# Tiles 1 to 3 of the mixer scanned in one pass, its output sums and the expert choices planned apart, a single tile's choice decoded in halves

## The reference, cut to what matters

```
y_ssd  = group_rmsnorm(y * silu(z)) @ ssd_w_out          # 8 groups of 256
y_sc   = (sb * causal_dwconv(sc * sx)) @ sc_w_out
merged = sigmoid(gates[:D]) * y_ssd + sigmoid(gates[D:]) * y_sc
h      = h + merged @ w_o
q = (rmsnorm(h) @ w_q)  -> 8 heads, 2 halves of 128
s = q . sub_keys        -> 128 scores per half; top 16 of each half,
                           then the top 16 of the 16 x 16 sums
eidx, g = indices and softmax of the 16 chosen (8 heads: 128 experts per token)
act = gelu(x . expert_u[eidx]);  h = h + sum(g * act * expert_v[eidx])
```

## Time and profile before

| | |
|---|---|
| median of three runs | 2622.79 us (2622.34 to 2625.23) |
| the profiled execution's own time | 2603.1 us |
| its span | 2601.3 us |
| TensorE busy | 2228.9 us (86%) |
| VectorE busy | 1518.6 us (58%) |
| GpSimd busy (gathers) | 1018.1 us (39%) |
| ScalarE busy | 686.5 us (26%) |
| moved by DMA | 869.29 MB, mean 334 GB/s |
| mean granted clock of TensorE | 0.924 of full speed |

### The profile page before, as it was taken

The page is one execution under the profiler, slowest core; times in us unless marked ns, Lnnn a source line. Parts: engine busy times, 40 slices in busy tenths (PEclk is TensorE's granted clock), DMA queues, the critical chain, the costliest instruction groups (busy, mean ns, idle before and its releaser), DMA issues.

```text
span 2601.3 us, 31972 instructions
## 1 busy us (share of the span) xinstructions
PE 2228.9 (86%) x11976; PEld 1677.5 (64%) x11976; DVE 1518.6 (58%) x3603; ACT 686.5 (26%) x2063; POOL 1018.1 (39%) x1028
## 2 busy tenths in 40 slices
PE   7999889988859999899868753468989799999998
PEld 7998778986758888678534133323365555546695
DVE  3441185854698998866643678841047678675210
ACT  6662245621225555400101010011022100001320
POOL 0000003333334564445456665666644556572000
PEclk9999999989879999899989977689997899999999
DMA  6556658999788998799999998999989999997375
GB/s 231 222 211 220 258 220 342 406 373 410 269 317 330 388 398 335 279 393 414 367 358 411 377 346 352 380 410 353 387 335 351 369 400 396 414 406 297 136 300 205
DMA packets 186091, 869.29 MB, mean 334 GB/s; under 512 B 20800, under 2 KB 21056, under 8 KB 153680
## 3 DMA queue, kind: packets, MB, share of 16 engines
q0 software_dynamic: 147456, 536.94, 53.4%
q1 hardware_dynamic: 37904, 328.20, 32.4%
q10 hardware_dynamic: 576, 2.10, 0.2%
HBM read 865.06 MB, written 2.10 MB: 333 GB/s over the span
## 4 chain that ended last, share of the span: by engine, by line
PE 69%; DVE 16%; issue 5%; ACT 4%; DMA 3%; another core or an unknown queue 2%; POOL 1%; DVEq 0%; ACTq 0%
PE ps L995 68%; DVE rows L2332 8%; POOL rows L975 1%; DMA rows<-in_pv,eidxT 1%; DMA wr<-in_wso 1%; ACT ynT L1631 1%; DVE si L1879 0%; PE ps L1340 0%; DVE tmpx L1965 0%; DVE h L2356 0%; PE ps L1104 0%; DMA wr<-in_wqku 0%; DVE late L1877 0%; DVE wb L2191 0%
## 5 line engine op out<-in xcount | busy, mean ns | idle before, releaser
L975 POOL DMA_INDIRECT rows<-in_pu,eidx x512 | 485.0, 947 | 982.1 <-DVE dots L2332 441.8
L2332 DVE CUSTOM_DVE_ANT_0 rows<-rows,ps 128x1024 f32<-128x1024 f32 x512 | 593.5, 1216 | 6.5 <-issue 5.9
L995 PE MATMUL ps<-uT,wr 128*128 128x128 f32 (+3 forms) x3456 | 553.6, 318 | 17.4 <-issue 11.1
L995 PEld LDWEIGHTS ps<-uT,wr 128*128 128x128 f32 x3456 | 502.6, 195 | 52.4 <-issue 18.9
L995 PE MATMUL ps<-hT,wr 128*128 128x128 f32 (+2 forms) x1600 | 363.9, 388 | 38.0 <-issue 34.2
L975 POOL DMA_INDIRECT rows<-in_pv,eidx x256 | 289.7, 1132 | 216.4 <-DVE h L2356 110.7
L995 PEld LDWEIGHTS ps<-hT,wr 128*128 128x128 f32 x1600 | 262.3, 199 | 135.5 <-issue 40.7
L975 POOL DMA_INDIRECT rows<-in_pv,eidxT x256 | 243.2, 950 | 144.8 <-issue 60.7
L995 PE MATMUL ps<-rows,wz 128*32 128x512 f32 x1024 | 207.8, 632 | 30.2 <-DMA rows<-in_pv,eidxT 24.4
L2356 DVE SCALAR_TENSOR_TENSOR h<-rows,wgt,h 128x1024 f32<-128x1024 f32 x132 | 169.1, 1281 | 5.0 <-DMA rows<-in_pv,eidx 4.1
L2356 DVE SCALAR_TENSOR_TENSOR ps<-rows,wgt,ps 128x1024 f32<-128x1024 f32 x122 | 156.7, 1285 | 11.2 <-DMA rows<-in_pv,eidx 10.9
(11 more groups left out here) (409 smaller groups left out, 2827.1 us busy)
## 6 DMA issues: line engine op xcount, KB each, us to landing
wr<-in_wg SPq DMA_DIRECT2D x48, 1536.0 KB
wr<-in_wsc SPq DMA_DIRECT2D x24, 1536.0 KB
wr<-in_wso SPq DMA_DIRECT2D x24, 1536.0 KB
wr<-in_wgu SPq DMA_DIRECT2D x33, 1024.0 KB
wr<-in_wgate SPq DMA_DIRECT2D x24, 1024.0 KB
wr<-in_wqku SPq DMA_DIRECT2D x15, 1024.0 KB
wr<-in_wo SPq DMA_DIRECT2D x12, 1024.0 KB
wr<-in_wdn SPq DMA_DIRECT2D x8, 1536.0 KB
```

The costliest lines, as they stand in the source:

```text
L975: e.indirect_dma_start(ring[i % NR], None, A[table], bass.IndirectOffsetOnAxis(ap=index[:, t, k:k + 1], axis=0)).then_inc(gathered[i % NR] ...
L995: return e.matmul(o, l, r, start=start, stop=stop, skip_group_check=True)
L2332: e.tensor_tensor_reduce(row, row, wide[:], 1.0, 0.0, MUL, ADD, dots[:, k:k + 1]).then_inc(*dve.up(*u))
```

## The change

- `SCANS = ((0, 1), (1, 4))`: tiles 1, 2 and 3 are scanned in one pass of 384 columns, over the weights of `in_wg` and `in_wsc` once. `GROUPS` keeps the three groups for the sums (`plan_sum`) and the choices.
- `scan(g)` goes chunk by chunk: `inside(c)` of one chunk, then `across(c - 1)` of the one before; its chunk buffers are two sets in turn (`c % 2`) in place of one per chunk, and `before_chunk` names the chunk whose reader must be done. z comes in two products (two chunks and one).
- The order: scan 0, sum 0, choice 0 merged with scan 1, sum 1, then choice 1 merged with sum 2, choice 2.
- In a sum, 4, 3 or 2 pairs of gate products (`AHEAD_GATES`) are made before the transposes, into as many buffers; both gates of a j share one bank and one sigmoid, both output products one bank and one multiplication. `yturn` fills a bank with four transposes. Queries and scores of a head come out of PSUM two at a time.
- `PIECES = (2, 2, 1)`: for tiles 0 and 1 the decoding is done for heads 0 to 3 after head 4's `top`, and for heads 4 to 7 at the end; a gather of the first 64 rows of expert_u waits for the first half alone.
- The scan of tiles 1 to 3 keeps some of its buffers in ring slots 8 to 12, as does choice 1. Until tile 1's choice is decoded the ring of rows has 8 slots, then 13. Working memory of the first block is one arena.
- Weight slots are 4 of 2304 values in place of 3 of 3072. `in_wg` comes in 3 pieces of 1 MB in place of 2 of 1.5 MB, `in_wsc` and `in_wso` in a piece of 1 MB and one of 0.5 MB, `in_wdn` in pieces of 4 (last 2) in place of 6 (last 4) rows of blocks. The pieces used at the end of the kernel have 4 slots more in place of 3.
- `QUOTA`, `CX`, `CY` and `SX` have other values.

```diff
-WSLOT = 3072
+WSLOT = 2304
-NW = 3
+NW = 4
-MIXERS = ((0, 1), (1, 2), (2, 4))
+SCANS = ((0, 1), (1, 4))
+GROUPS = ((0, 1), (1, 2), (2, 4))
-SX = 1.6
-PLACES = ("early", "beside", "ring")
-CX = 3.1
-CY = 1.7
+SX = 1.8
+PLACES = ("early", "ring", "ring")
+CX = 5.3
+CY = 4.4
+NR0 = 8
+AHEAD_GATES = (4, 3, 2)
+GATE_BUFFERS = (4, 3, 2)
+PIECES = (2, 2, 1)
-QUOTA = {('mixer', 1, 1): 17, ('mixer', 1, 2): 19, ('late', 1): 6, ('sum', 1): 26, ('mixer', 2, 0): 66, ('mixer', 2, 1): 62, ('mixer', 2, 2): 39, ('sum', 2): 82, ('query', 2): 98, ('top', 3): 65, ('attend', 0): 142, ('heads', 0): 64, ('wout', 0): 42, ('attend', 2): 20, ('heads', 2): 19, ('wout', 2): 4, ('feed', 0): 20, ('feed', 0, 0): 28, ('feed', 0, 1): 34, ('feed', 0, 2): 49, ('down', 0, 0): 35, ('down', 0, 1): 100, ('top', 2): 0, ('query', 1): 14, ('late', 2): 20, ('feed', 0, 3): 8, ('top', 0): 0, ('mixer', 1, 0): 0}
+QUOTA = {('query', 2): 108, ('top', 3): 72, ('attend', 0): 128, ('heads', 0): 66, ('wout', 0): 53, ('attend', 2): 20, ('heads', 2): 10, ('wout', 2): 8, ('feed', 0): 13, ('feed', 0, 0): 39, ('feed', 0, 1): 23, ('feed', 0, 2): 50, ('down', 0, 0): 25, ('down', 0, 1): 130, ('top', 2): 3, ('query', 1): 10, ('feed', 0, 3): 21, ('top', 0): 0, ('mixer', 1, 0): 0, ('mixer', 1, 1): 33, ('mixer', 1, 2): 34, ('mixer', 1, 3): 31, ('mixer', 1, 4): 28, ('mixer', 1, 5): 31, ('mixer', 1, 6): 35, ('mixer', 1, 7): 27, ('mixer', 1, 8): 3, ('late', 1): 5, ('sum', 1): 22, ('late', 2): 9, ('sum', 2): 74, ('top', 1): 5}
...
+def before_chunk(q, g, c):
+    n = len(group(*SCANS[q])[4])
+    if c >= 2:
+        return g, c - 2
+    return (g - 1, c + 2 * ((n - 1 - c) // 2)) if g else None
...
+        slopes(0)
+        slopes(1)
+        for c in range(nc_ + 1):
+            if c < nc_:
+                yield from inside(c)
+            if c:
+                yield from across(c - 1)
...
+    for j in range(AHEAD_GATES[q]):
+        yield from gate_products(j)
+    for i in range(4 * nt):
+        pl.take(("yturn", q, i), "lo", ("act", "yturn", q, i))
...
+    def decoded(t, h):
+        if PIECES[q] == 2 and h == 4:
+            yield from decode(t, 0)
...
-        yield from mixer[0]
-        yield from turns(mixer[1], choose[0])
-        yield from merge(pl, (choose[0], 0.001), (mixer[1], CX))
-        yield from turns(mixer[2], choose[1])
-        yield from merge(pl, (choose[1], 0.001), (until("clear", mixer[2]), CY))
-        yield from mixer[2]
+        yield from scan[0]
+        yield from sums[0]
+        yield from turns(scan[1], choose[0])
+        yield from merge(pl, (choose[0], 0.001), (scan[1], CX))
+        yield from sums[1]
+        pl.rings.update(lo=(0, 1), hi=(3, 4))
+        yield from merge(pl, (choose[1], 0.001), (sums[2], CY))
+        pl.rings.update(lo=(0, 1, 2), hi=(3, 4, 5))
         yield from choose[2]
...
-                w.wait_ge(*(act.at("index", t) if kind == "row" else dve.at("chosen", t)))
+                if kind == "row":
+                    w.wait_ge(*act.at("index", t))
+                else:
+                    w.wait_ge(*dve.at("chosen", t, 0 if kind == "dot" and k < 64 else pieces_of(t) - 1))
...
                 elif kind == "xdt":
+                    old = before_chunk(q, g, c)
+                    if old is not None:
+                        w.wait_ge(*pe.at("outer" if group(*SCANS[q])[4][old[1]][2] is None else "y", q, *old))
```

More of the change, by code:

```diff
@@ L107, in __init__ @@
         self.units, self.bank, self.slot, self.loads = [], {}, {}, []
-        self.held = {"ring": [], "early": [], "beside": [], "last": []}
+        self.held = {"ring": [], "early": [], "last": []}
         self.turns = ("ring",)
-        self.rings = {"lo": (0, 1, 2, 3), "hi": (4, 5, 6, 7), "six": (6,), "seven": (7,)}
+        self.rings = {"lo": (0, 1, 2, 3), "hi": (4, 5, 6, 7), "two": (2,), "five": (5,)}
         self.turn = {k: 0 for k in self.rings}
@@ L136, in load @@
         k = len(held)
-        first, n_ = {"ring": (0, NW), "early": (NW, 3), "beside": (NW + 3, 2), "last": (NW + 5, 3)}[place]
+        first, n_ = {"ring": (0, NW), "early": (NW, 3), "last": (NW + 3, 4)}[place]
         old = held[k - n_] if k >= n_ else ("dve", "h2e", NT - 1) if place == "last" else None
@@ L254, in scan, with slopes, inside @@
     def scan(g):
-        real = [(c, col, k) for c, (col, w_, k) in enumerate(chunks) if k is not None]
-        pl.add("slopes", q, g)
-        for c, (col, w_, k) in enumerate(chunks):
+        def slopes(c):
+            if c < nc_ and chunks[c][2] is not None:
+                pl.add("slopes", q, g, c)
+        def inside(c):
+            col, w_, k = chunks[c]
             pl.take(("back", q, g, c), "hi", ("act", "xdt", q, g, c))
@@ L843, in build @@
+        ob = ring[9:9 + NT]
+        wr += [rows[:, WSLOT * i:WSLOT * i + WSLOT] for i in range(4)]
         with ExitStack() as pk:
@@ L933, in build @@
         job_of = {u: i for i, u in enumerate(jobs)}
+        consumers = ("dot", "vrow", "rows")
+        narrow = NR0 + sum(2 if u[0] == "rows" else 1 for u in pl.units[:pl.units.index(("chosen", 1, 1, PIECES[1] - 1))]
+                           if u[0] in consumers)
+        slots, user, slot_of, before_of, value_of = [7, 5, 6, 0, 1, 2, 3, 4], {}, [], [], []
+        for i in range(len(jobs)):
+            if i == narrow:
+                slots = list(range(NR0, NR)) + slots
+            s = slots.pop(0)
+            slots.append(s)
+            slot_of.append(s)
+            before_of.append(user.get(s))
+            value_of.append(16 if user.get(s) is None else value_of[user[s]] + 16)
+            user[s] = i
         def sync(e):
@@ new lines, in gpsimd, with known @@
+            w.wait_ge(*pe.at("turn", ("mix", 0), SCANS[0][1]))
+            issued, chosen, used = 0, set(), -1
+            def known(i):
+                kind, t, k = jobs[i][0:3]
+                return (t, 0 if kind == "dot" and k < 64 else pieces_of(t) - 1) in chosen
+            for u in pl.units:
+                if u[0] == "chosen":
+                    chosen.add(u[2:4])
+                elif u[0] in consumers:
+                    used = job_of[("row", u[1], u[2], 2 * u[3] + 1) if u[0] == "rows" else u]
+                else:
+                    continue
+                while issued < len(jobs) and known(issued) and (
+                        before_of[issued] <= used if before_of[issued] is not None else
+                        slot_of[issued] < NR0 or (1, PIECES[1] - 1) in chosen):
+                    gather(issued)
+                    issued += 1
@@ L2110, in vector @@
                 elif kind == "slots":
-                    _, q, t = u
+                    _, q, t, piece = u
                     m = CH[q]
-                    i = t - MIXERS[q][0]
-                    cx, first, rd = m["cx1"], m["cx0"], m["rd"]
-                    gt = gate[:, t, :].rearrange("p (h k) -> p h k", h=8)
-                    unit, place, last, second = (m[f"cy{i_}"] for i_ in range(4))
+                    i = t - GROUPS[q][0]
+                    hs = heads_of(q, piece)
+                    mine = lambda nm: m[nm][:, 0:hs.stop - hs.start]
```

876 lines of the change are left out of this document (454 added, 422 removed).

## The result

The changed kernel took 2555.49 us (median of four runs, 2549.31 to 2565.66), the kernel before beside it 2624.01 us (2622.34 to 2626.77): ratio 0.9746, 95% interval 0.9717 to 0.9776. It is 68.5 us faster. The forecast was 2544, its range 2490 to 2610. (The median before is 2624.01 here and was 2622.79 in the prediction, because a fourth run came in.)

The account below looks back on a forecast made before the run. The prediction took TensorE and whatever makes it stop as the bound. Its terms -3 -95 -20 +12 +27 gave -79 us, so 2622.8 became 2544 us, with a whole range of 2490 to 2610.

Parts of the forecast that it names:

- Start to choice 0, -3: Start to 300 us: unchanged but for four gate pieces made ahead of tile 0's normalisation, -3 us (0 to -8).
- One scan, periods of 57.6: Scan of tiles 1 to 3: eight groups at TensorE's pace, each 57.6 us in place of 58.2.
- Sum of tile 1 ... I take 102, -20: Sum of tile 1: from 122 to 102 us, -20, bounds 92 and 122.
- Scans with choice 0, 613 to 518: Choice 0 and scans, with choice 1 moved out: 613 us become 518, -95, of which 493 is TensorE work.
- Sum 2 with choice 1, 242: Sum of tiles 2 and 3 with choice 1 inside: 230 us without it become 242, +12, bounds 206 and 260.
- Choice 2, +27: Choice 2, 258 us before: 20 rows missing at its start are made up there, +27 us, bounds 0 and +35.
- From 1523 on, 0: First attention stage and what follows: the same 1078 us, taken as 0 within -15 to +10.
- Saved traffic given back: Rival: DMA idles once tile 0's rows are finished and pays later in the sums and choice 2; 2582 us, chance 0.26.
- Everything packs: Rival: from 388 to 1523 us TensorE's work fills 95% of the time, saving 127 us; 2495 us, chance 0.14.
- The scan waits on its own chunks: Rival: two chunk buffer sets serve three chunks, stopping TensorE up to 4.0 us per chunk; 2640 us, chance 0.10.
- No change: Rival: the first attention stage waits for tile 1's last row, which comes no sooner; 2623 us, chance 0.06.
- near 1440: Sign of being right: the first attention stage would start near 1440 us.

Follow-up runs that it names:

- e6_rows_kept: Changed kernel with 28 rows of tile 0 moved from the scan to the start of the sum of tiles 2 and 3; 2504.65 us against 2483.67 unaltered, chip 10.
- e2_seek_late: Changed kernel, rows of tiles 0 and 1 sought only after both halves of the choice are decoded; 2564.03 us against 2556.34 unaltered, chip 5.
- e12_sum_light: Changed kernel with 20 rows moved from the sum of tiles 2 and 3 into choice 2; 2578.90 us against 2552.65 unaltered, chip 6.
- first pair: First traces of the kernel before and the changed kernel, medians 2624.01 and 2555.49 us; the second pair traces both kernels on chip 6, 2614.20 and 2552.65.
- e7_three_slots: Changed kernel with three weight slots of 2304 values in place of four; 2514.29 us against 2483.67 unaltered, chip 10.
- e4_traffic: Changed kernel with each weight piece of the scan of tiles 1 to 3 also copied memory to memory; 2588.48 us against 2556.34 unaltered, chip 5.
- e3_choice_alone: Changed kernel with choice 1 planned ahead of the sum of tiles 2 and 3, not beside it; 2570.28 us against 2556.34 unaltered, chip 5.
- e1_again: Changed kernel run again unaltered on chip 5; 2556.34 us against 2611.16 for the kernel before.
- e10_again: Changed kernel run again unaltered on chip 6; 2552.65 us against 2614.20 for the kernel before.

## Why the prediction came out as it did

The direction was right and the time in the range, 11 us above the forecast. That it came so near was partly luck: by its own steps one error of 48 us met others of the opposite sign.

- *Start to choice 0, -3.* It ended at 298.40 against 298.59: 0.
- *One scan, periods of 57.6.* 57.43. 58.2 - 57.43 = 0.8 us was saved in a group, where the constant of the rows had said 0.6 for 112 instructions; the order inside a group changed too, so the other 0.2 has no one cause. The prediction misread its own rows beside the page: by the Trainium skill's formula ("TensorE: Matmul & The Clock Gate", Back-to-back issue gap), N/2.4 ns plus 2.5 ns, an instruction of 128 columns would be spaced 0.056 us, and the earlier trace rows have 0.112. An estimate with that page's gap taken twice gives 0.112, 0.218 and 0.325 us, and the rows have 0.112, 0.216 and 0.322. So taken, the trace agrees with the page, and 112 x 5 ns = 0.6 us a group is the very term that the sum used; it is not 2 us, and no larger gap of small products is needed.
- *The failed step: "Sum of tile 1 ... I take 102, -20", and with it the cut of the windows.* The old windows were cut 18.3 us and 29.6 us ahead of the two scans' ends. The new lengths of both sums were then built from the sums' own work, 92 and 206 us of TensorE. So 47.9 us of scan (39.2 of them TensorE work, 14.1 + 25.1) stood on the side of before and nowhere on the side of after. At the true joint sum 1 was 104.1 us long, not 122, and it became 110.0: +6, not -20. The three arrivals of weights in the earlier trace rows, 29 us together, were steps of the chain and not idle time of TensorE: TensorE was busy 94.2 of those 104.1 us and waited for DMA 3.5 us in all.
- *Scans with choice 0, 613 to 518.* With the 47.9 us put back 518 is 566, with TensorE's part of it alone 557; measured 547.6, so here the step was 10 to 18 us too careful.
- *Sum 2 with choice 1, 242.* Measured 243.0, and the reason is not borne out, so this was luck too. The sum put 29 us on rows that cannot be sought; e6_rows_kept leaves some 3 for that. TensorE has 214.7 us of work there, not 206, and stops: 11 us behind `merged`, which stands behind VectorE's owed products and decoding. This stop is 17 us when rows are sought later (e2_seek_late) and 7 when fewer are laid there (e12_sum_light).
- *Choice 2, +27.* +31.5 and +26.7. The count of the 20 missing rows was right (165 and 185 gathers in the stage); that each costs 1.35 us is less than the 2.2 of e12_sum_light; why the total fits all the same was not tried.
- *From 1523 on, 0.* 1066.8 for 1069.5 in the first pair, 1080.1 for 1067.6 in the second. The fourth slot is worth nothing there, as taken (1029.0 and 1029.1 in e7_three_slots), and 31 us before it, which the prediction did not price: it took it for granted that the sums stay fed.

With the 47.9 us put back the sum of the prediction is -31, and the profiled execution would become 2572; it was 2565.7. The second error was the step from one execution to the median: 19.7 us were added as if fixed. For the kernel before that was right (2603.1 and 2624.0), for the changed one the profiled execution stands 10 us over its median. So the missing 48 us were offset by 30 us of this kind and by the 18 us of care in the scans; the 11 us that remained are the smaller misses, sum 1 (+8), choice 2 (+4), the start (+3) and sum 2 (+1) against the rest (-3), and 2 us of rounding at the window edges.

The rivals. *Saved traffic given back*: it did not come true as a whole, for putting the traffic back costs 32 to 41 us of the 55 to 61 that the change gains on those two chips (the copies' own writes are in that figure). Its sum 1 without gain and its +27 in choice 2 did come true. *Everything packs*: the scan does (421 of 428 us), the sums and choice 2 do not. *The scan waits on its own chunks*: not with two sets of buffers at this traffic; the periods are 57.43 us, and TensorE's waits in 408 to 846 come to some 15 us in all, 8.5 of them in one place, where the rival had 79 to 96. *No change*: the first attention product came 35 us sooner. Of the marks named ahead, "near 1440" for that stage failed (1481 by its turning, 1496.7 by its first product), for the 48 us.

What the gain is made of: on chip 5 the traffic is worth some 32 us (e4_traffic) and choice 1's place beside the sum 15 (e3_choice_alone), together 47 of 55, if the two add up, which was not tried; neither was run on chip 10, where the whole gain is 21.

What stays open: where the 15 to 30 us between executions of one kernel go, since only one execution of each set has a trace (in e1_again, the first trace and e10_again, all the changed kernel, the stretch from `att` to the end is 1059.5, 1066.8 and 1080.1 us); what the single parts of the change are worth by themselves beyond those tried; and whether a version with more rows in the sum of tiles 2 and 3 (the opposite of e12_sum_light) would beat the changed kernel. It was not run.

## What to carry to other kernels

Cut stages at the last product of their kind, and check that the work of all new stages adds up to that of the old ones: TensorE had 862 us from choice 0's turn to choice 2's, the steps remove 17, and the new stages of the prediction held 493 + 92 + 206 = 791, which is 54 short (39 by the misplaced window edges, the rest by sums taken too light); 832 was measured. When a stage looks starved of data, ask first whether the engine that consumes the data has room: in e6_rows_kept rows laid into the idle DMA time held up VectorE's next step, and TensorE for 29.6 us with it. A step that reads DMA in the chain of waits is not yet a stop of an engine; look up what the engine itself waited. Take the spread of executions into the step from one profile to a median, and know which end of it the profile is.

## What had not been expected of the hardware

The same two kernels took 2611 and 2556 us on one chip, 2613 and 2553 on another, and 2505 and 2484 on a third: the change is worth 55, 61 or 21 us. TensorE's periods are the same 57.4 to 57.5 us on all of them. What differs in the traces is the DMA rate once gathers and weights are in flight together behind the scan, 409 to 414 GB/s in most slices on the third and 278 to 411 on the others. That the rate makes the difference is argued from this. Each chip served for one set of runs only, so a slower chip and other work on the same memory at that time are not told apart. Gathers of 512 KB beside weight pieces of 1 MB ran at those 409 to 414 GB/s. The Trainium skill ("DMA: Bandwidth & Descriptors", Bandwidth) asks for at least 1 MiB per transfer and has 341 GB/s at 1 MB; 14 slices of chip 10, where many transfers are in flight at once, do not bear that out for them.
